# Three more groups of gate and up as seven block products each, in three feed-forward layers of a two-layer decoder trunk

## What is computed

```python
def swiglu(x, w_gate, w_up, w_down):
    return (jax.nn.silu(x @ w_gate) * (x @ w_up)) @ w_down

def half_ffn(h, l, j):
    y = swiglu(rms_norm(h, ffn_norm_pre[l, j]), ffn_w_gate[l, j], ffn_w_up[l, j], ffn_w_down[l, j])
    return h + 0.5 * rms_norm(y, ffn_norm_post[l, j])
```

## Time and profile before

| | before |
|---|---|
| median of 3 runs | 2297.38 us (2297.29 to 2299.59) |
| the profiled execution's own time | 2296.25 us |
| its span, first to last instruction | 2294.2 us |
| TensorE busy | 2263.9 us, 99% of the span |
| VectorE busy | 1483.9 us, 65% |
| ScalarE busy | 1049.5 us, 46% |
| granted TensorE clock, mean share | 0.998 |
| moved by DMA | 249.84 MB, 109 GB/s over the span |

### The profile page before, as it was taken

The page is one execution under the profiler, slowest core; times in us unless marked ns, Lnnn a source line. Parts: engine busy times, 40 slices in busy tenths (PEclk is TensorE's granted clock), DMA queues, the critical chain, the costliest instruction groups (busy, mean ns, idle before and its releaser), DMA issues. The chain is left out here.

```text
span 2294.2 us, 32607 instructions
## 1 busy us (share of the span) xinstructions
PE 2263.9 (99%) x12963; PEld 1969.6 (86%) x12963; DVE 1483.9 (65%) x1913; ACT 1049.5 (46%) x1627; POOL 103.3 (5%) x145
## 2 busy tenths in 40 slices
PE   8999999999999999999999999999999999999998
PEld 7888888888888888889988889988878888888997
DVE  5757445586545658577757567746896575756774
ACT  5433324444544444436544435535265554343552
POOL 0000003100000000000010000000000000000000
PEclk9999999999999999999999999999999999999999
DMA  4342332321223233415534315543322213431562
GB/s 169 104 135 74 99 106 73 113 68 59 74 74 101 65 127 131 142 51 140 167 126 166 124 42 147 166 156 92 101 75 83 92 65 98 150 124 59 132 173 110
DMA packets 181757, 249.84 MB, mean 109 GB/s; under 512 B 13832, under 2 KB 125800, under 8 KB 181608
## 3 DMA queue, kind: packets, MB, share of 16 engines
q1 hardware_dynamic: 177176, 232.00, 31.2%
q0 software_dynamic: 4320, 15.73, 3.5%
q10 hardware_dynamic: 112, 0.03, 0.0%
HBM read 222.54 MB, written 9.44 MB: 101 GB/s over the span
## 5 line engine op out<-in xcount | busy, mean ns | idle before, releaser
L2476 PE MATMUL ps<-xlo,whi 128*128 128x512 f32 (+1 forms) x1936 | 671.0, 347 | 7.7 <-issue 5.7
L2478 PE MATMUL ps<-xhi,whi 128*128 128x512 f32 (+1 forms) x1936 | 668.1, 345 | 0.0
L2477 PE MATMUL ps<-xhi,wlo 128*128 128x512 f32 (+1 forms) x1696 | 600.3, 354 | 0.0
L1532 DVE TENSOR_TENSOR wlo<-raw,whi 128x1024 fp32r<-128x1024 f32 x251 | 306.3, 1224 | 321.4 <-ACT whi L916 318.6
L916 ACT ACTIVATE whi<-raw 128x1024 fp32r<-128x1024 f32 x281 | 294.9, 1054 | 342.9 <-PE ps L2478 301.1
L2476 PEld LDWEIGHTS ps<-xlo,whi 128*128 128x128 f32 x1936 | 367.5, 190 | 53.2 <-issue 9.2
L2478 PEld LDWEIGHTS ps<-xhi,whi 128*128 128x128 f32 x1936 | 367.3, 190 | 44.1
L2477 PEld LDWEIGHTS ps<-xhi,wlo 128*128 128x128 f32 x1696 | 321.4, 190 | 43.6
L1538 DVE SCALAR_TENSOR_TENSOR wlo<-raw,vec,whi 128x512 fp32r<-128x512 f32 (+1 forms) x224 | 154.7, 735 | 154.2 <-ACT whi L920 153.6
L920 ACT ACTIVATE whi<-raw,vec 128x512 fp32r<-128x512 f32 (+1 forms) x224 | 145.4, 702 | 197.9 <-PE ps L2478 163.2
L2476 PE MATMUL ps<-wlo,xhi 128*128 128x512 f32 x352 | 138.7, 394 | 1.0 <-issue 1.0
(11 more groups left out here) (323 smaller groups left out, 3829.7 us busy)
## 6 DMA issues: line engine op xcount, KB each, us to landing
raw<-ffn_w_gate_dram SPq DMA_DIRECT2D x176, 256.0 KB, 3.1
raw<-ffn_w_up_dram SPq DMA_DIRECT2D x176, 256.0 KB, 3.2
raw<-ffn_w_down_dram SPq DMA_DIRECT2D x96, 256.0 KB, 2.9
w<-ffn_w_down_dram SPq DMA_DIRECT2D x72, 256.0 KB, 5.3
raw<-xattn_w_kv_dram SPq DMA_DIRECT2D x64, 256.0 KB, 3.0
lo_aside<-raw POOLq DMA_DIRECT2D x30, 512.0 KB, 5.1
raw<-even_w_in_dram SPq DMA_DIRECT2D x56, 256.0 KB, 2.9
raw<-odd_w_in_dram SPq DMA_DIRECT2D x42, 256.0 KB, 2.9
```

The source lines that it names most:

```text
L1532: v.tensor_tensor(flat(wlo[:, slot]), flat(raw[:, from_slot]), flat(whi[:, slot]).bitcast(f32), SUB).then_inc(lo_made, 1)
L2476: mm(out_ap, lh, rl, start=start, stop=False, skip_group_check=skip_group_check)
L2477: mm(out_ap, ll, rh, start=False, stop=False, skip_group_check=skip_group_check)
L2478: return mm(out_ap, lh, rh, start=False, stop=stop, skip_group_check=skip_group_check)
```

## The change

1. `WOVEN` takes in groups 3, 4 and 5, so the second stage of three SwiGLUs is made of products too. The first stage and the SwiGLU (0, 0) stay plain.
2. c12 moves from `mid` to a place of its own in the last quarter of `ring`. ACT's wait for the low parts of the product before (`mid_lo_ready`) moves from the copy of c12 to the last silu, which now is the first to write `mid`.
3. DVE's early sums of the down weights, which stood after the four pieces of plain group 5, are put inside woven group 5: t1 before T3's low part, t2 before c22, t3 before c12, t4 before the last product. A `split_next` that the plain group had before its block sums is kept for the woven one.
4. In the closings before gate and up ACT squares tile 1 ahead of scaling tile 0.

The order of SP's loads is as it was: the corner loads still stand behind the first three raw loads of group 4.

```diff
-WOVEN = (6, 7, 8, 9, 10)
+WOVEN = (3, 4, 5, 6, 7, 8, 9, 10)
...
+    c12 = place("c12", [P, 2, HALF], f32, ring_at + 3 * SEQ * FLOAT)
...
                 next_h(0)
+                square_tile(kind, second, 1, done + n)
                 scale_rows(0)
-                square_tile(kind, second, 1, done + n)
...
             keep(1, c22[:], z_out)
             split_next()
-            act.wait_ge(mid_lo_ready, 2 * (mids - 1))
-            keep(2, c12, x_out)
+            keep(2, c12[:], x_out)
...
             act.wait_ge(pieces_used, base + len(WOVEN_UNITS) + SPLIT_SLOTS)
+            act.wait_ge(mid_lo_ready, 2 * (mids - 1))
             a(c21, x_out, ACT.Silu).then_inc(gate_silu, 1)
...
-        def weave(w, group, mids, held_mid):
+        def weave(w, group, mids, held_mid, next_pass):
...
                 else:
                     block_low(g, held)
+            if next_pass is not None:
+                t1_sums(next_pass)
             split_next()
...
             v.tensor_tensor(c11[:], y_out, c11[:], ADD).then_inc(c11_ready, 1)
             split_next()
+            if next_pass is not None:
+                t2_sums(next_pass, 0, late)
             dve.wait_ge(product_kept, 3 * w + 2)
             unit_done("T3")
             v.tensor_tensor(c22[:], x_out, c22[:], ADD).then_inc(c22_ready, 1)
             split_next()
+            if next_pass is not None:
+                t3_sums(next_pass, 0, late)
             dve.wait_ge(product_kept, 3 * w + 3)
             unit_done("B22")
-            E.run(v.tensor_tensor(c12, z_out, c12, ADD))
+            E.run(v.tensor_tensor(c12[:], z_out, c12[:], ADD))
...
-            v.tensor_tensor(u12, c11[:], c12, MUL)
+            v.tensor_tensor(u12, c11[:], c12[:], MUL)
             split_next()
+            if next_pass is not None:
+                t4_sums(next_pass, 0, late)
             dve.wait_ge(gate_silu, mids).then_inc(bank_free[bank // 4], 1)
...
                     if woven(kind, l, arg, g):
+                        if g == ng - 1 and not plain:
+                            split_next()
                         E.group += 1
```

More of the change, by code:

```diff
@@ L1219, in weave @@
             x_out, z_out = [PS[:, b, :].rearrange("p (f n) -> p f n", f=2) for b in (bank, bank + 2)]
-            c12, c21 = halves_of(mid[:, 0:4, :], 0), halves_of(mid[:, 4:8, :], 1)
+            c21 = halves_of(mid[:, 4:8, :], 1)
             def keep(unit, dst, src):
@@ L2020, in token_sums @@
                 low(S_MADE[step - 7])
-        def weave(w, group, mids, held_mid):
+        def weave(w, group, mids, held_mid, next_pass):
             base, bank = woven_base[w], 4 * (group % 2)
             x_out, y_out, z_out = [PS[:, bank + b, :].rearrange("p (f n) -> p f n", f=2) for b in range(3)]
-            c12, u12 = halves_of(mid[:, 0:4, :], 0), halves_of(mid[:, 4:8, :], 0)
+            u12 = halves_of(mid[:, 4:8, :], 0)
             c21 = halves_of(mid[:, 4:8, :], 1)
@@ L2080, in _ @@
                         mids += 1
-                        weave(woven_group[n_stage, g], E.group, mids, held_mid)
+                        weave(woven_group[n_stage, g], E.group, mids, held_mid, pass_of.get(after) if g == ng - 1 else None)
                     for kp in range(0 if woven(kind, l, arg, g) else 4):
```

## The result

| | before | after |
|---|---|---|
| median | 2297.34 us (2296.37 to 2299.59, 4 runs) | 2321.76 us (2319.24 to 2325.53, 4 runs) |
| ratio | | 1.0104, 95% interval 1.0091 to 1.0116 |
| profiled execution, span | 2294.2 us | 2317.4 us |
| granted TensorE clock, mean | 0.998 | 0.993 |

The change makes the kernel 24.4 us slower. 2309 was forecast, with a range up to 2321: the sign and most of the waits came out as put, the size was twice what was put.

A forecast was written before the change was run, and what follows sets the result against it. TensorE (PE), busy 2263.9 of 2294.2 us, was taken to bound the kernel. Per layer 9.3 us lost against 4.8 won, 13.5 slower over three layers, less 1.5 in the closings: 12.0 slower, 2309 us, range 2291 to 2321.

The forecast's parts named there:

- Step 1: PE's work: nine groups turn from plain to products, 14.4 us less in all, 4.8 per layer.
- Step 2: Group 4: nine corner loads in the raw-load burst delay B21's landing by 3.2 us, so T2 waits; 3.5 us lost per layer.
- rival D: Worse burst: corner transfers at 190 to 300 GB/s, B21 lands 6 us later, 14.1 lost per layer, 2324 us; chance 0.15.
- Step 2, the queue: B11's accumulating transfer starts only when loads issued before it are through; taking turns at once would make the sum 2 us smaller.
- Steps 3 and 4: DVE's c22 late for group 4's T4, 1.0 us; B11's transfer late for group 5's start, 2.2 us; both per layer.
- Step 5: Down-weight sums inside group 5 make c22 late for T4, 2.2 us, and a PSUM bank late in the quads, 0.4, per layer.
- Step 6: Group 3, group 6 and the first woven stage: nothing lost; the moved c12 and moved wait cost nothing.
- Step 7: Closings: squaring tile 1 before scaling tile 0 shortens PE's waits, 1.5 us gained in all.
- B: Corner loads find room in the burst's gaps: 4.4 us lost against 4.8 won per layer, 2295 us; chance 0.20.
- C: DVE's order does not bind, c22 in group 5 is in time: 2.5 us gained per layer, 2288 us; chance 0.13.
- A: The sum of the steps as put: 9.3 us lost against 4.8 won per layer, 2309 us; chance 0.52.

The follow-up runs named there:

- e12: The changed kernel with only group 3 of the stage as products, groups 4 and 5 plain, corner loads as before the change: 2293.68 us, 0.9980 of before.
- e6: The changed kernel with idle matmuls for PE in group 4, 12 ahead of B11 and 16 ahead of T2: 2322.94 us, 1.0098 of before.
- e5: The kernel before with only the new order in the closings (tile 1 squared ahead of scaling tile 0): 2298.05 us, 0.9995 of before.
- e11: The changed kernel with groups 3 and 4 as products, group 5 plain, and the corner loads placed as in e7: 2296.72 us, 0.9991 of before.
- e3: The changed kernel with DVE's down-weight sums moved: t1 to group 4's end, t2 behind c22, t4 behind the last product: 2316.21 us, 1.0075 of before.
- e4: The changed kernel with e3's moved sums and the corner loads issued early, behind group 3's last raw load: 2303.96 us, 1.0016 of before.
- e7: The changed kernel with e3's sums, corners w11 and w12 behind the landing of group 3's B11, w21 behind group 4's last raw load: 2300.48 us, 1.0003.
- e8: e7 with SP holding B12's raw load in woven groups but a stage's first until ACT has negated B11: 2342.57 us, 1.0185 of before.
- e10: The kernel before with B12's raw load held until ACT has negated B11, in groups 7 to 10 of its woven stages: 2328.64 us, 1.0121.

## Why the prediction was wrong in size

Times here count from the start of group 3, mean of the three layers of after.

- **Step 1** right: PE has 13611 matmuls for 12963, 648 more, which is 1512 of 256 columns more and 864 of 512 fewer, and e12 shows 1.58 us per group.
- **Step 2** is the step that failed: "the landing is at 24.1, T2 can start at 29.4, and group 4 loses 3.5". ACT's wait for the last raw load ended at 25.6, 25.6 and 26.0, and T2 started at 30.85, 30.84 and 31.23, mean 31.0. The loss is 31.0 - 25.9 = 5.1, not 3.5: 1.6 a layer, 4.7 in all. It is the largest of the misses, and under half of the 11.2 us by which the span is off. ACT's part was right (5.2 for 5.3); the delay of the landing was not: in the first layer it was 4.7 against t = 20.9, where 3.2 was taken, inside the bounds of 2.1 to 6.0. The burst did start earlier, at 947.72 or 7.0 us in where 8.1 was today's, so the corner loads really cost 5.8: the idle 28% of the earlier trace rows took up next to nothing of them. The estimate by 393 GB/s gave 6.0 and was right as it stood; what was taken off for the room in the burst was not there. The whole mix ran at 269 GB/s with 87% of the engines' time used, which lies in rival D's 190 to 300, but what the corner loads added went at 2.36 MB in 5.8 us, some 407 GB/s, and not at D's rate.
- **Step 2, the queue**: the reading of rows 9, that B11's transfer starts when the loads issued before it are through, does not hold. After, in the first layer, it was issued at 953.88, and from 957.6 to 961.6 its packets (q0) and those of SP's loads (q1) ran side by side:

```profile
q0 software_dynamic: 144, 0.52, 65.7%
q1 hardware_dynamic: 517, 0.55, 40.8%
```

  A load issued ahead of it, at 953.46, took 8.2 us and landed at the end of that stretch. Nor did it start at once: its first packet came 3.8 us after its issue, and comes after 1.4 in a transfer that has the queue to itself. Loads behind it and loads ahead of it both cost it time.
- **Steps 3 and 4** together: group 5 starts at 49.1, which is 49.1 - 31.0 - 14.4 = 3.7 of loss where 1.0 + 2.2 were put; some of it is PE's half clock, since without that (e6) it is 48.6 - 31.2 - 14.4 = 3.0.
- **Step 5**: group 5's T4 starts 66.3, 69.8 and 68.6 in, 68.3 - 49.1 - 17.3 = 1.9 of loss; 2.2 was put. In the quads 0.77 a layer instead of 0.4, 1.1 us more in all, and not by the release of a bank: PE waits for DVE's low part of a corner (`wlo`, L1524), 0.3 us by the view, 17.6 into the pass.
- **Step 6**, nothing in the other stages: they show 3.0 more, within the scatter of kernels that change nothing there, so no cause is claimed. Within the stage group 3's T4 waited 0.84 and 1.08 in two layers, inside the 5.1.
- **Step 7**: the waits shrank by 1.2 (1.5 put), all of it in the closing of `down`, where 1.6 became 0.4. The rest of the kernel is nevertheless level (+0.1), for a reason ahead of everything that the change touches: a stretch at half clock at 581 us lasted 10.24 us where before had 3.41, which cost 2.8 us; and before had one of 3.41 at 14 us that after lacks, which had cost before 1.6. The first was 10.24 in most of the kernels run, that of e5 among them; what sets it is not known.

Sum: 12.0 put + 4.7 (step 2) + 1.6 (steps 3, 4) - 1.0 (step 5 in the stage) + 1.1 (quads) + 3.0 (step 6) + 1.6 (step 7 and the clock elsewhere) = 23.0 of 23.2. Of the rivals, B and C are refuted; A and D are one mechanism with two prices of the burst. D's time (2324) came closer, but by luck: its sign, a stage over 74 us, was not seen (69.3, 72.8, 71.6), stage and quads lost (17.9 + 2.3 + 14.4) / 3 = 11.5 us a layer, between A's 9.3 and D's 14.1, and what brought the time near 2324 was groups 6 to 10 and the clock elsewhere, which D does not name.

Not settled: how much of the 3.0 in groups 6 to 10 the change causes, and how much of e11's missing gain beyond the 7.5 us of its stage is the kernel's. A low part of B11 made other than by DMA was not tried.

## To carry to other kernels

When an engine that is never idle gets less work, the gain is what remains after the chain of its suppliers is laid out for the new, shorter period: look at each queue's order, not its busy share (DVE was at 65%). A load moved into a burst can delay everything behind it by its whole transfer time, as 5.8 us for 2.36 MB here, and the last piece of the burst is the one to follow. Try one unit of a repeated change before all: here one group of three kept its gain whole, and all three with the best placing found were level with none.

## What the runs showed of the hardware

- The granted clock fell to 0.50 for 3.4 or 6.8 us in or within 1.5 us behind waits of 2.4 to 3.7 us in the changed stage, in e3, e4 and e7 also behind waits of 1.9 to 2.0; behind the 3.05 of after's second layer and the 2.6 of e6 it did not fall. And those stretches cost nothing of their own where PE was to wait for its suppliers next (e6).
- An accumulating transfer of 512 KB took 4.4 us alone, mostly 6.3 to 7.0 with 1.0 to 1.5 MB of loads issued about as early (e8, e10), 6.3 to 8.7 with such loads ahead of it (before), and 7.4 to 9.5 in groups 4 and 5 of after. By the Trainium skill ("DMA: Bandwidth & Descriptors", Queues, rings and completion order) an engine takes turns between its queues; the case of e8 and e10 agrees, and so does the stretch above in which both queues ran, while the last two show that work issued earlier costs it more.
- A wait cost PE some 0.15 us more than the view of waits gives: there a matmul of 256 columns ends 0.28 us after its start, and the next one starts 0.12 after it when there is no wait.
